# First norm: the last piece of a chunk on TensorE behind the column sums, and VectorE's pieces between tiles of h

## The chip, the cores and the metric
One core of a Trainium2 chip runs the whole program. The time is device microseconds from start to end of the program on that core; lower is better.

## The reference, cut to what matters
One layer of a hybrid decoder (256 tokens, width 2048, all float32). The part around the change is the modulation and the first norm:

```python
c_act = jax.nn.silu(c)
mod = c_act @ w_ada[l] + b_ada[l]
sh1, sc1, g1, sh2, sc2, g2 = [m[:, None, :] for m in jnp.split(mod, N_MOD, axis=-1)]
h = rms_norm(x, norm1_w[l]) * (1.0 + sc1) + sh1
proj = h @ w_in[l]
...
x = x + g1 * y_mix
h = rms_norm(x, norm2_w[l]) * (1.0 + sc2) + sh2
...
return rms_norm(x, final_norm_w)
```

`sh1` and `sc1` are a vector of 2048 times a matrix of 2048 x 4096: 32 MB that are read once and needed before the first product with `w_in` can begin.

## The kernel before
Float32 products are made of three faster ones: a weight tile is split into `whi` (ScalarE, `hi_part`) and `wlo` (VectorE, `lo_part`, `first_lo`), and h likewise, so that a unit of 256 x 512 weights is 24 matmuls on TensorE (12 of twice the width for token units). Weights come through a ring of four buffers.

The first norm is made in four chunks of 512 columns. For a chunk c the shift and scale need 16 pieces of `w_ada`, r = 0 to 15, each 128 rows x 1024 columns (shift and scale side by side, 512 KB), in a ring of 12 buffers `pc`; the DMA queue of SP brings them in order, with six units of `w_in` between. Most pieces are added on VectorE by `first_piece`: it multiplies the piece by 128 values of silu(c), one per partition, and adds it to `acc_c` (semaphore `s_pcd`). The pieces in `PE_TILES[c]` are multiplied on TensorE instead, as eight one-column matmuls with the piece as the stationary operand, accumulated in a bank (`s_pcp`). When VectorE has added its last piece, `chunk_columns(c)` on TensorE sums `acc_c` over its partitions, eight more one-column matmuls into the same bank, and sets `s_red`. VectorE's `chunk(c)` then makes the shift and the scale, ScalarE's `chunk_hi` makes `htmp0` and the high part of h for four tiles, and VectorE the low part of each.

Each chunk of h allows six units of the projections. TensorE runs units 0 to 3 of a chunk, each followed by one of its pieces of the next chunk, then the columns of the next chunk behind unit 3, and then units 4 and 5, which cover the making of the next four tiles of h. VectorE's order is written out by hand too: pieces with a `lo_part` behind r = 2, 4, 8, 11 and 15. SP issues in order and waits for a buffer's last reader. In chunk 0 there are no units yet; TensorE has the transposes of x and of parameters instead.

The lines that the text names: L886 is a piece on TensorE, L895 the column sums, L930 to L945 matmuls of units, L1320 and L1323 a piece on VectorE (the first one of a chunk, the others), L1330 to L1332 the norm's shift and scale, L1336 the low part of h, L1311 and L1340 `wlo`.

Of the kernel before, what the change touches and what calls it, by code (L numbers as in the profile page):

```python
# [17 lines left out]
KT = D // P  # L18
# [26 lines left out]
CHUNKS, CT = 4, 4  # L45
# [5 lines left out]
def unit_of(u):  # L51

    if u < EARLY_UNITS:
        return u % PER_CHUNK // 2, u // PER_CHUNK * 2 + u % 2
    return u // 8, u % 8
# [4 lines left out]


PC_RING = 12
PE_TILES = ((2, 5, 8, 11), (1, 5, 9, 13), (1, 5, 9, 13), (1, 5, 9, 13))
PC_OF_PE = [c * KT + r for c in range(CHUNKS) for r in PE_TILES[c]]
PC_OF_DVE = [i for i in range(CHUNKS * KT) if i not in PC_OF_PE]
OUT0, UP0 = PROJ_UNITS, PROJ_UNITS + 32
# [123 lines left out]
def build(nc, x, c, positions, w_ada, b_ada, norm1_w, w_in, lb_logits, gnorm_w, w_out,  # L190
# [6 lines left out]
    with ExitStack() as ctx:  # L197
# [3 lines left out]
        def sem(name):  # L201
            return ctx.enter_context(nc.semaphore(name))
# [79 lines left out]
        csilu = small[:, 0:16]  # L282
# [32 lines left out]
        s_pcp = sem("s_pcp")  # L315
# [92 lines left out]
        def ev(n):  # L408

            return 2 * n + 2  # L410
# [460 lines left out]
        def _(pe):  # L871
# [6 lines left out]
            def first_piece(i):  # L878

                c, r = i // KT, i % KT  # L880
                pe.wait_ge(s_pc[i % PC_RING], (i // PC_RING + 1) * 16)
                if r == PE_TILES[c][0]:
                    if c >= 2:
                        pe.wait_ge(s_redc, c - 1)
                for k in range(2 * CT):
                    last = pe.matmul(ps[6 + c % 2][:, k:k + 1], pc[:, i % PC_RING, k // CT, k % CT * P:(k % CT + 1) * P],  # L886
                                     csilu[:, r:r + 1], start=(r == PE_TILES[c][0] and k == 0), stop=False,
                                     skip_group_check=True)
                last.then_inc(s_pcp, 1)

            def chunk_columns(c):

                pe.wait_ge(s_pcd, sum(i < (c + 1) * KT for i in PC_OF_DVE))
                for k in range(2 * CT):
                    last = pe.matmul(ps[6 + c % 2][:, k:k + 1], acc_c[:, c % 2, k * P:(k + 1) * P], ones[:, 0:1],  # L895
                                     start=False, stop=True, skip_group_check=True)
                last.then_inc(s_red, 1)

            pe.wait_ge(s_csilu, 1)
            first_piece(2)  # L900
            for k in range(KT // 2):
                if k >= 4:
# [12 lines left out]
            for t in range(4):  # L915
                last = pe.transpose(ps[1][:, 97 + 88 * t:97 + 88 * (t + 1)], rows[0:88, 1 + t, :], ident[0:88, 0:88])
            last.then_inc(s_prmT, 1)
            first_piece(11)
            chunk_columns(0)
            pe.wait_ge(s_xTc, KT // 2)  # L920
            pe.wait_ge(s_prm, 3)

            def channel_unit(n, j, slot):

                for f in range(4):
                    out = ps[BANK[n] + f // 2][:, f % 2 * SEQ:(f % 2 + 1) * SEQ]
                    cols = slice(f * P, (f + 1) * P)
                    for k in range(UK):
                        kk = j * UK + k
                        pe.matmul(out, whi[:, slot, k, cols], h[:, kk, 0, :], start=(kk == 0 and f % 2 == 0), stop=False,  # L930
                                  skip_group_check=True)
                        pe.matmul(out, whi[:, slot, k, cols], h[:, kk, 1, :], start=False, stop=False, skip_group_check=True)  # L932
                        last = pe.matmul(out, wlo[:, slot, k, cols], h[:, kk, 0, :], start=False, stop=(kk == KT - 1),  # L933
                                         skip_group_check=True)
                last.then_inc(s_pe, 1)

            def token_unit(bank0, j, slot, hi, lo, tiles, early=None):
                for b in range(TB):
                    out, tok = ps[bank0 + b], slice(b * P, (b + 1) * P)
                    for k in range(UK):  # L940
                        kk = tiles + k
                        first, end = j == 0 and k == 0, j == 7 and k == UK - 1
                        pe.matmul(out, hi(kk, tok), whi[:, slot, k, :], start=first, stop=False)  # L943
                        pe.matmul(out, hi(kk, tok), wlo[:, slot, k, :], start=False, stop=False)  # L944
                        last = pe.matmul(out, lo(kk, tok), whi[:, slot, k, :], start=False, stop=end)  # L945
                    if early and b == 0:
                        last.then_inc(early, 1)
                last.then_inc(s_pe, 1)
# [163 lines left out]
            for u in range(PROJ_UNITS):  # L1112
                n, j = unit_of(u)
                if j == 0 and n >= EARLY:
                    pe.wait_ge(s_ev, ev(n - EARLY if n < 5 else n - 2))
                pe.wait_ge(s_lo, u + 1)
                if n < EARLY:
                    pe.wait_ge(s_h, UK * (j + 1))
                if GROUPS[n][0] in ("hi", "av", "hg"):
                    token_unit(BANK[n], j, u % RING, lambda kk, tok: h[:, kk, 0, tok], lambda kk, tok: h[:, kk, 1, tok], j * UK)  # L1120
                else:
                    channel_unit(n, j, u % RING)
                if u < EARLY_UNITS - PER_CHUNK:
                    c, t = u // PER_CHUNK + 1, u % PER_CHUNK
                    if t < 4:
                        first_piece(c * KT + PE_TILES[c][t])
                    if t == 3:
                        chunk_columns(c)
                after(u)

            def mix_hi(kk, tok):
# [127 lines left out]
        def _(dve):  # L1259
# [47 lines left out]
            def lo_part(unit, slot, ready):  # L1307

                dve.wait_ge(s_hi, unit)
                dve.wait_ge(s_pe, ready)  # L1310
                dve.tensor_tensor(wlo[:, slot], wraw[:, slot], whi[:, slot].bitcast(F32), ALU.subtract).then_inc(s_lo, 1)  # L1311

            def first_piece(i):
                c, r = i // KT, i % KT
                dve.wait_ge(s_pc[i % PC_RING], (i // PC_RING + 1) * 16)
                a, new = acc_c[:, c % 2], pc[:, i % PC_RING].rearrange("p m n -> p (m n)")
                if r == 0:
                    if c >= 2:
                        dve.wait_ge(s_red, c - 1)
                    ins = dve.tensor_scalar(a, new, csilu[:, r:r + 1], None, ALU.mult)  # L1320
                else:
                    dve.wait_ge(s_pcd, PC_OF_DVE.index(i))
                    ins = dve.scalar_tensor_tensor(out=a, in0=new, scalar=csilu[:, r:r + 1], in1=a, op0=ALU.mult, op1=ALU.add)  # L1323
                ins.then_inc(s_pcd, 1)

            def chunk(c):

                cols, sums = slice(CT * c, CT * c + CT), ps[6 + c % 2]
                dve.wait_ge(s_red, c + 1)
                st.do(dve.tensor_tensor(B1[:, cols], sums[:, 0:CT], b_shift[:, cols], ALU.add))  # L1330
                st.then(dve.tensor_tensor(acol, sums[:, CT:2 * CT], b_scale[:, cols], ALU.add))
                dve.tensor_tensor(A1[:, cols], acol, n1w[:, cols], ALU.mult).then_inc(s_redc, 1)  # L1332
                for k in range(CT * c, CT * c + CT):
                    dve.wait_ge(s_ht, k + 1)
                    dve.wait_ge(s_hhi, k + 1)
                    dve.tensor_tensor(h[:, k, 1, :], htmp0[:, k % 2], h[:, k, 0, :].bitcast(F32), ALU.subtract).then_inc(s_h, 1)  # L1336

            def first_lo(v):
                dve.wait_ge(s_hi, v + 1)
                dve.tensor_tensor(wlo[:, v], wraw[:, v], whi[:, v].bitcast(F32), ALU.subtract).then_inc(s_lo, 1)  # L1340

            dve.wait_ge(s_csilu, 1)
            for r in range(KT):
                if r not in PE_TILES[0]:
                    first_piece(r)
# [14 lines left out]
            for c in range(CHUNKS - 1):  # L1360
                v = PER_CHUNK * c
                for r in range(KT):
                    if r not in PE_TILES[c + 1]:
                        first_piece((c + 1) * KT + r)
                    if r in (2, 4, 8, 11, 15):
                        e = (2, 4, 8, 11, 15).index(r) + 2
                        if v + e < RING:
                            first_lo(v + e)
                        else:
                            lo_part(v + e + 1, (v + e) % RING, v + e - RING + 1)  # L1370
                lo_part(v + 8, (v + 7) % RING, v + 7 - RING + 1)
                if c == 1:
                    bound_logits()
                elif c == 2:
                    bound()
                chunk(c + 1)
# [368 lines left out]
```

## Time and profile before

| | us |
|---|---|
| median of 3 runs | 1317.16 (1315.12 to 1317.34) |
| profiled execution, its own time | 1316.54 |
| span of the profile | 1314.7 |
| TensorE busy | 1269.4 (97%) |
| VectorE busy | 997.6 (76%) |
| ScalarE busy | 608.1 (46%) |

The span is what the engines' records cover; the profiled execution's own time has 1.84 us around it. Busy shares are means over the whole program. The change touches only what happens in the first 135 us, so the timelines there are what is to be read. A matmul's duration in a row has the draining of its last result in it, so rows that follow each other overlap by some 0.15 us; sixteen records stand for eight float32 matmuls, in two passes each.

### The profile page before, as it was taken

The page shows a single profiled execution, that of the slowest core. Times are in us where ns is not written, and L with a number is a line of the kernel's source. Part 1 is how long each engine was busy: PE and PEld are TensorE (multiplying, and loading weights), DVE is VectorE, ACT ScalarE, POOL GpSimd, SP SyncE. Part 2 cuts the span into 40 slices and gives each one's busy share as a digit, 9 for nine tenths or more (in the row PEclk, how much of TensorE's full clock was granted, in tenths as well). Part 3 has the DMA queues.
Part 4 walks back from the last instruction along what each step waited for, and adds up shares of the span by engine and source line. Part 5 has one row for each costly group of instructions (what it writes and reads, how often), then busy time and mean ns, then how long its engine had stood idle before and what let it go on. Part 6 is the DMA issues. An engine that isn't in the chain of part 4 may idle for free.

```text
span 1314.7 us, 20785 instructions
## 1 busy us (share of the span) xinstructions
PE 1269.4 (97%) x7298; PEld 1119.3 (85%) x7298; DVE 997.6 (76%) x1278; ACT 608.1 (46%) x793; POOL 51.3 (4%) x99
## 2 busy tenths in 40 slices
PE   4799999999999999989999999999999999999997
PEld 4799999998998878878888888888888878888886
DVE  3788698998888889787878797888777765545454
ACT  3333654444545654454444444444444444434342
POOL 2000000032121000000000000000000000000000
PEclk9788999999999999989999999999999999999999
DMA  9999788888778799749777777777666675555553
GB/s 339 387 385 367 244 299 273 262 275 273 251 254 304 261 341 386 273 152 305 233 240 235 241 226 240 237 238 211 192 189 190 189 259 193 194 195 194 194 195 116
DMA packets 151715, 329.77 MB, mean 251 GB/s; under 512 B 11237, under 2 KB 11990, under 8 KB 150754
## 3 DMA queue, kind: packets, MB, share of 16 engines
q1 hardware_dynamic: 148000, 318.49, 73.1%
q0 software_dynamic: 3360, 9.98, 2.2%
q8 instruction: 40, 0.66, 0.2%
q10 hardware_dynamic: 290, 0.44, 0.1%
q14 instruction: 25, 0.20, 0.0%
HBM read 323.09 MB, written 4.19 MB: 249 GB/s over the span
## 4 chain that ended last, share of the span: by engine, by line
PE 89%; DVE 4%; DMA 3%; ACT 2%; issue 1%; SPq 1%; DVEq 0%; ACTq 0%
PE bank L1182 25%; PE bank L1188 13%; PE bank L1207 6%; PE bank L1209 6%; PE bank L1208 6%; PE bank L943 5%; PE bank L945 5%; PE bank L944 5%; PE bank L930 4%; PE bank L933 4%; PE bank L932 4%; DMA pc<-in_w_ada 3%; DVE acc_c L1323 1%; PE bank L977 1%; PE bank L964 1%
## 5 line engine op out<-in xcount | busy, mean ns | idle before, releaser
L624 ACT ACTIVATE whi<-wraw 128x1024 fp32r<-128x1024 f32 x408 | 432.0, 1060 | 630.1 <-PE bank L1188 238.9
L1311 DVE TENSOR_TENSOR wlo<-wraw,whi 128x1024 fp32r<-128x1024 f32 x404 | 494.0, 1224 | 252.3 <-ACT whi L624 250.8
L1182 PE MATMUL bank<-h,whi 128*128 128x512 f32 x1400 | 351.0, 392 | 0.0
L1182 PEld LDWEIGHTS bank<-h,whi 128*128 128x128 f32 x1400 | 252.2, 189 | 45.2
L1188 PEld LDWEIGHTS bank<-h,wlo 128*128 128x128 f32 x1400 | 191.0, 190 | 13.7
L1188 PE MATMUL bank<-h,wlo 128*128 128x256 f32 x1400 | 195.2, 282 | 0.0
L930 PE MATMUL bank<-h,whi 128*128 128x256 f32 x512 | 149.2, 291 | 3.3 <-DVE h L1336 3.3
L932 PE MATMUL bank<-h,whi 128*128 128x256 f32 x512 | 146.4, 286 | 0.0
L933 PE MATMUL bank<-h,wlo 128*128 128x256 f32 x512 | 146.3, 286 | 0.0
L1207 PE MATMUL bank<-whi,act_hi 128*128 128x512 f32 x336 | 130.8, 389 | 0.3 <-DVE evt L1599 0.3
L1209 PE MATMUL bank<-whi,act_lo 128*128 128x512 f32 x336 | 130.7, 389 | 0.0
L1208 PE MATMUL bank<-wlo,act_hi 128*128 128x512 f32 x336 | 130.7, 389 | 0.0
L1387 DVE SCALAR_TENSOR_TENSOR acc<-araw,small,acc 128x1024 f32<-128x1024 f32 x96 | 122.7, 1279 | 0.5 <-issue 0.3
L930 PEld LDWEIGHTS bank<-h,whi 128*128 128x128 f32 x512 | 99.8, 195 | 3.6 <-issue 3.4
L932 PEld LDWEIGHTS bank<-h,whi 128*128 128x128 f32 x512 | 99.9, 195 | 0.2
L933 PEld LDWEIGHTS bank<-h,wlo 128*128 128x128 f32 x512 | 99.7, 195 | 0.0
L943 PE MATMUL bank<-whi,h 128*128 128x512 f32 x192 | 81.2, 423 | 0.0
L945 PE MATMUL bank<-whi,h 128*128 128x512 f32 x192 | 77.1, 401 | 0.0
L944 PE MATMUL bank<-wlo,h 128*128 128x512 f32 x192 | 76.9, 400 | 0.0
L1207 PEld LDWEIGHTS bank<-whi,act_hi 128*128 128x128 f32 x336 | 63.1, 188 | 14.1 <-issue 1.1
L1208 PEld LDWEIGHTS bank<-wlo,act_hi 128*128 128x128 f32 x336 | 63.1, 188 | 13.2
L1209 PEld LDWEIGHTS bank<-whi,act_lo 128*128 128x128 f32 x336 | 63.1, 188 | 13.0
(233 smaller groups left out, 1325.9 us busy)
## 6 DMA issues: line engine op xcount, KB each, us to landing
wraw<-in_w_up SPq DMA_DIRECT2D x176, 512.0 KB, 4.4
araw<-in_w_ada SPq DMA_DIRECT2D x128, 512.0 KB, 5.6
wraw<-in_w_in SPq DMA_DIRECT2D x112, 512.0 KB, 4.9
wraw<-in_w_down SPq DMA_DIRECT2D x88, 512.0 KB, 4.1
pc<-in_w_ada SPq DMA_DIRECT2D x64, 512.0 KB, 11.4
wraw<-in_w_out SPq DMA_DIRECT2D x32, 512.0 KB, 6.0
x<-in_x SPq DMA_DIRECT2D x2, 1024.0 KB, 7.1
x<-in_x POOLq DMA_DIRECT2D x1, 2048.0 KB, 11.4
```

The source lines that it names most:

```text
L624: act.activation(whi[:, slot], wraw[:, slot], ACT.Copy).then_inc(s_hi, 1)
L930: pe.matmul(out, whi[:, slot, k, cols], h[:, kk, 0, :], start=(kk == 0 and f % 2 == 0), stop=False, skip_group_check=True)
L932: pe.matmul(out, whi[:, slot, k, cols], h[:, kk, 1, :], start=False, stop=False, skip_group_check=True)
L933: last = pe.matmul(out, wlo[:, slot, k, cols], h[:, kk, 0, :], start=False, stop=(kk == KT - 1), skip_group_check=True)
L943: pe.matmul(out, hi(kk, tok), whi[:, slot, k, :], start=first, stop=False)
L945: last = pe.matmul(out, lo(kk, tok), whi[:, slot, k, :], start=False, stop=end)
L1182: pe.matmul(ps[bank0 + f], whi[:, slot, k, f * P:(f + 1) * P], h[:, kk].rearrange("p a t -> p (a t)"), start=(kk == 0), stop=False, skip_g ...
L1188: last = pe.matmul(ps[bank0 + f][:, 0:SEQ], wlo[:, slot, k, f * P:(f + 1) * P], h[:, kk, 0, :], start=False, stop=(kk == KT - 1), skip_gro ...
L1207: pe.matmul(ps[bank0 + b], hi(kk, b), whi[:, slot, k, :], start=first, stop=False)
L1208: pe.matmul(ps[bank0 + b], hi(kk, b), wlo[:, slot, k, :], start=False, stop=False)
L1209: last = pe.matmul(ps[bank0 + b], lo(kk, b), whi[:, slot, k, :], start=False, stop=end)
L1311: dve.tensor_tensor(wlo[:, slot], wraw[:, slot], whi[:, slot].bitcast(F32), ALU.subtract).then_inc(s_lo, 1)
```

## The change
The pieces of TensorE are now 2, 5, 8, 15 in chunk 0 and 1, 5, 9, 15 in the others. In chunk 0 VectorE adds piece 11 and in the others piece 13, where TensorE did, and TensorE takes piece 15, where VectorE did. TensorE's last piece stands behind `chunk_columns`, no longer ahead of it. `chunk(c)` waits for that piece as well (`s_pcp`). VectorE adds piece 0 of the next chunk between tiles 1 and 2 of h, and piece 2 behind tile 3, ahead of everything else of the next chunk.

```diff
-PE_TILES = ((2, 5, 8, 11), (1, 5, 9, 13), (1, 5, 9, 13), (1, 5, 9, 13))
+PE_TILES = ((2, 5, 8, 15), (1, 5, 9, 15), (1, 5, 9, 15), (1, 5, 9, 15))
...
-                                     csilu[:, r:r + 1], start=(r == PE_TILES[c][0] and k == 0), stop=False,
+                                     csilu[:, r:r + 1], start=(r == PE_TILES[c][0] and k == 0), stop=(r == PE_TILES[c][-1]),
...
-                                     start=False, stop=True, skip_group_check=True)
+                                     start=False, stop=False, skip_group_check=True)
...
-            first_piece(11)
             chunk_columns(0)
+            first_piece(15)
...
+                    if t == 3:
+                        chunk_columns(c)
                     if t < 4:
                         first_piece(c * KT + PE_TILES[c][t])
-                    if t == 3:
-                        chunk_columns(c)
...
                 dve.wait_ge(s_red, c + 1)
+                dve.wait_ge(s_pcp, 4 * c + 4)
...
                     dve.tensor_tensor(h[:, k, 1, :], htmp0[:, k % 2], h[:, k, 0, :].bitcast(F32), ALU.subtract).then_inc(s_h, 1)
+                    if c + 1 < CHUNKS and k % CT in (1, 3):
+                        first_piece((c + 1) * KT + k % CT - 1)
...
-                    if r not in PE_TILES[c + 1]:
+                    if r not in PE_TILES[c + 1] and r not in (0, 2):
                         first_piece((c + 1) * KT + r)
```

What stands on TensorE in chunk 0 between the transposes of the parameters (L916) and the first unit, before (`s_pc11` is the landing of piece 11; `s_pcd` VectorE's sums):

```order
L886 MATMUL bank<-small,pc 128x1 [waits s_pc8]
L886 MATMUL bank<-small,pc 128x1 x7
L916 MATMUL bank<-ident,rows 128x88 [waits s_prm,s_in]
L916 MATMUL bank<-ident,rows 128x88 x3
L886 MATMUL bank<-small,pc 128x1 [waits s_pc11]
L886 MATMUL bank<-small,pc 128x1 x7
L895 MATMUL bank<-ones,acc_c 128x1 [waits s_pcd]
L895 MATMUL bank<-ones,acc_c 128x1 x7
```

The same place on TensorE now (`s_pc3` is the landing of piece 15):

```order
L886 MATMUL bank<-small,pc 128x1 [waits s_pc8]
L886 MATMUL bank<-small,pc 128x1 x7
L916 MATMUL bank<-ident,rows 128x88 [waits s_prm,s_in]
L916 MATMUL bank<-ident,rows 128x88 x3
L895 MATMUL bank<-ones,acc_c 128x1 [waits s_pcd]
L895 MATMUL bank<-ones,acc_c 128x1 x7
L886 MATMUL bank<-small,pc 128x1 [waits s_pc3]
L886 MATMUL bank<-small,pc 128x1 x7
```

The piece that stood ahead of the wait for VectorE is gone, and another stands behind the columns.

TensorE behind unit 3, ahead of the columns of chunk 1, before (`s_pc5` is piece 13 of that chunk):

```order
L933 MATMUL bank<-h,wlo 128x256
L886 MATMUL bank<-small,pc 128x1 [waits s_pc5]
L886 MATMUL bank<-small,pc 128x1 x7
L895 MATMUL bank<-ones,acc_c 128x1 [waits s_pcd]
L895 MATMUL bank<-ones,acc_c 128x1 x7
L943 MATMUL bank<-whi,h 128x512 [waits s_h,s_lo]
```

And now (`s_pc7` is piece 15 of that chunk):

```order
L933 MATMUL bank<-h,wlo 128x256
L895 MATMUL bank<-ones,acc_c 128x1 [waits s_pcd]
L895 MATMUL bank<-ones,acc_c 128x1 x7
L886 MATMUL bank<-small,pc 128x1 [waits s_pc7]
L886 MATMUL bank<-small,pc 128x1 x7
L943 MATMUL bank<-whi,h 128x512 [waits s_h,s_lo]
```

The wait for VectorE's sums now follows the unit at once, and the piece lies between the columns and unit 4.

VectorE from the last pieces of chunk 0 to the first of chunk 1, before (`s_pc2` and `s_pc3` are pieces 14 and 15 of chunk 0, `s_pc4` and `s_pc6` pieces 0 and 2 of chunk 1):

```order
L1323 SCALAR_TENSOR_TENSOR acc_c<-pc,small,acc_c 128x1024 [waits s_pcd,s_pc2]
L1340 TENSOR_TENSOR wlo<-wraw,whi 128x1024 [waits s_hi]
L1323 SCALAR_TENSOR_TENSOR acc_c<-pc,small,acc_c 128x1024 [waits s_pcd,s_pc3]
L1340 TENSOR_TENSOR wlo<-wraw,whi 128x1024 [waits s_hi]
L1330 TENSOR_TENSOR small<-bank,small 128x4 [waits s_red,s_xTc]
L1331 TENSOR_TENSOR small<-bank,small 128x4
L1332 TENSOR_TENSOR small<-small,prm 128x4 [waits s_v]
L1336 TENSOR_TENSOR h<-htmp_64,h 128x256 [waits s_hhi,s_ht] x4
L1320 TENSOR_SCALAR acc_c<-pc,small 128x1024 [waits s_pc4]
L1323 SCALAR_TENSOR_TENSOR acc_c<-pc,small,acc_c 128x1024 [waits s_pcd,s_pc6]
```

The same place now:

```order
L1323 SCALAR_TENSOR_TENSOR acc_c<-pc,small,acc_c 128x1024 [waits s_pcd,s_pc2]
L1343 TENSOR_TENSOR wlo<-wraw,whi 128x1024 [waits s_hi] x2
L1331 TENSOR_TENSOR small<-bank,small 128x4 [waits s_pcp,s_red,s_xTc]
L1332 TENSOR_TENSOR small<-bank,small 128x4
L1333 TENSOR_TENSOR small<-small,prm 128x4 [waits s_v]
L1337 TENSOR_TENSOR h<-htmp_64,h 128x256 [waits s_hhi,s_ht] x2
L1320 TENSOR_SCALAR acc_c<-pc,small 128x1024 [waits s_pc4]
L1337 TENSOR_TENSOR h<-htmp_64,h 128x256 [waits s_hhi,s_ht] x2
L1323 SCALAR_TENSOR_TENSOR acc_c<-pc,small,acc_c 128x1024 [waits s_pcd,s_pc6]
```

Piece 15 is gone from the row of sums, the norm waits for `s_pcp` too, and piece 0 of the next chunk stands in the middle of the four tiles of h.

## Rows read from the trace of the kernel before

**Rows 1.** The page, busy time of TensorE, share of the span, instructions.
```profile
PE 1269.4 (97%) x7298; PEld 1119.3 (85%) x7298; DVE 997.6 (76%) x1278; ACT 608.1 (46%) x793; POOL 51.3 (4%) x99
```

**Rows 2.** TensorE's waits, 0 to 160 us: total, times, longest.
```profile
PE bank L895 <- DVE acc_c L1323: 5.6, 3, 3.9
PE bank L930 <- DVE h L1336: 3.3, 1, 3.3
```

**Rows 3.** TensorE's timeline, chunk 0: start, duration, instruction, idle before and its releaser.
```profile
30.66 3.63 PE L886 MATMUL bank<-small,pc 128*128 128x1 f32 x32
...
34.49 2.69 PE L886 MATMUL bank<-small,pc 128*128 128x1 f32 x16
41.04 3.57 PE L895 MATMUL bank<-ones,acc_c 128*128 128x1 f32 x16 [3.86 <-DVE acc_c L1323]
47.93 0.55 PE L930 MATMUL bank<-h,whi 128*128 128x256 f32 x1 [3.32 <-DVE h L1336]
```

**Rows 4.** VectorE's timeline, end of chunk 0 and beginning of chunk 1.
```profile
33.34 2.67 DVE L1323 SCALAR_TENSOR_TENSOR acc_c<-pc,small,acc_c 128x1024 f32<-128x1024 f32 x2 [2.76 <-DMA pc<-in_w_ada]
...
37.37 1.28 DVE L1323 SCALAR_TENSOR_TENSOR acc_c<-pc,small,acc_c 128x1024 f32<-128x1024 f32 x1 [0.92 <-DMA pc<-in_w_ada]
...
39.70 1.28 DVE L1323 SCALAR_TENSOR_TENSOR acc_c<-pc,small,acc_c 128x1024 f32<-128x1024 f32 x1
...
48.34 0.43 DVE L1336 TENSOR_TENSOR h<-htmp,h 128x256 fp32r<-128x256 f32 x1 [0.56 <-ACT h L657]
...
49.66 0.75 DVE L1320 TENSOR_SCALAR acc_c<-pc,small 128x1024 f32<-128x1024 f32 x1
50.52 1.28 DVE L1323 SCALAR_TENSOR_TENSOR acc_c<-pc,small,acc_c 128x1024 f32<-128x1024 f32 x1
```

**Rows 5.** Windows of one microsecond: engines' busy time, then clock, DMA share, GB/s.
```profile
35.00:36.00 1.00, 1.00 (x9) 1.00 (x8) 1.00 (x2) 0.00 (x0) 0.00 (x0) 0.67 1.05 387
...
69.00:70.00 1.00, 0.07 (x1) 0.08 (x1) 1.00 (x2) 0.74 (x1) 0.00 (x0) 0.73 1.05 399
...
76.00:77.00 1.00, 1.00 (x5) 0.80 (x4) 0.42 (x1) 1.00 (x4) 0.00 (x0) 0.85 1.07 393
...
100.00:101.00 1.00, 1.00 (x7) 1.00 (x8) 1.00 (x2) 0.00 (x0) 0.00 (x0) 0.59 1.04 383
...
107.00:108.00 1.00, 1.00 (x5) 0.82 (x5) 0.92 (x1) 0.99 (x3) 0.00 (x0) 0.99 1.05 387
...
130.00:131.00 1.00, 1.00 (x8) 0.92 (x8) 0.97 (x3) 0.00 (x0) 0.00 (x0) 0.95 0.53 90
...
134.00:135.00 1.00, 1.00 (x6) 0.77 (x5) 0.42 (x1) 1.00 (x3) 0.71 (x2) 0.84 0.55 209
```

**Rows 6.** TensorE's timeline, the columns of chunks 1, 2 and 3.
```profile
66.82 1.84 PE L886 MATMUL bank<-small,pc 128*128 128x1 f32 x16
69.93 3.58 PE L895 MATMUL bank<-ones,acc_c 128*128 128x1 f32 x16 [1.26 <-DVE acc_c L1323]
73.36 0.77 PE L943 MATMUL bank<-whi,h 128*128 128x512 f32 x1
...
97.14 1.84 PE L886 MATMUL bank<-small,pc 128*128 128x1 f32 x16
98.85 2.34 PE L895 MATMUL bank<-ones,acc_c 128*128 128x1 f32 x16
...
126.22 1.84 PE L886 MATMUL bank<-small,pc 128*128 128x1 f32 x16
128.53 1.95 PE L895 MATMUL bank<-ones,acc_c 128*128 128x1 f32 x16 [0.47 <-DVE acc_c L1323]
```

**Rows 7.** VectorE's timeline, the last pieces of chunk 1 and of chunk 3.
```profile
65.81 4.06 DVE L1323 SCALAR_TENSOR_TENSOR acc_c<-pc,small,acc_c 128x1024 f32<-128x1024 f32 x3
...
125.81 2.67 DVE L1323 SCALAR_TENSOR_TENSOR acc_c<-pc,small,acc_c 128x1024 f32<-128x1024 f32 x2 [1.42 <-DMA pc<-in_w_ada]
```

**Rows 8.** SP's queue, issues of pieces 8 to 11 of chunk 2.
```profile
74.05 6.07 SPq L439 DMA_DIRECT2D pc<-in_w_ada  x4
```

## The prediction
> **What bounds the kernel now.** I read the page first: TensorE is busy 97% of the span [rows 1], so what counts is when its continuous work begins and what is lost inside it. Next the waits of TensorE up to 160 us [rows 2]: after the start it waits four times, three times for the sums on VectorE ahead of `chunk_columns` (5.6 us, longest 3.9) and once for the first tiles of h (3.3 us). The timelines give their places. In chunk 0 the pieces 5 and 8 run at full speed, piece 11 is the last of TensorE's work (done at 37.18), then it sits idle 3.86 us, takes 3.57 us for the column sums and idles 3.32 us more until h is there at 47.93 [rows 3]. In chunk 1 it idles 1.26 us by the bracket (1.4 us by its rows, 68.5 to 69.93), in chunk 3 0.47 us; in chunk 2 the columns start with no wait [rows 6]. From 47.93 on everything else is work, so a microsecond by which unit 0 or a later resumption moves is a microsecond of the end.
>
> VectorE is paced by landings in chunk 0: it waits for pieces 12 and 14 [rows 4], and each piece lands 1.35 us behind the one before (524 KB at 387 GB/s, [rows 5]). In chunk 1 it is late and paced by its own work: its last three pieces run back to back to 69.87 [rows 7], while piece 15 had landed about 22 transfers behind piece 14 of chunk 0, at 37.4 + 22 x 1.35 = 67.1.
>
> The third thing to see is the granted clock. It fell (shares of one-microsecond rows worked out) at 35.3, 69.5, 100.2 and 130.9, and was full again at 76.3, 107.0 and 134.3 [rows 5]. Ahead of each fall TensorE had left its wide matmuls for one-column ones: pieces at 30.66 [rows 3], 66.82, 97.14 and 126.22 [rows 6]. So it fell 4.7, 2.6, 3.0 and 4.7 us after they ended. At 35.3 it had not been idle at all. At full speed eight one-column matmuls take 1.7 us of the queue, at half 3.43 (69.93 to 73.36, [rows 6]).
>
> **The change part by part.** Pieces of VectorE: twelve a chunk before and after; it loses 15 and gets 11 or 13. TensorE has four a chunk, as before. The `stop` flags are no instructions; I cost them at nothing.
>
> *Chunk 0.* Piece 11 moves into VectorE's idle 2.76 us ahead of 33.34 [rows 4]: 1.28 us of work, covered. (Uncovered it would cost 1.28.) Its last piece is now 14, which starts on its landing at 37.37 and ends at 38.65; the columns began 0.06 us behind the last sum, so they start at 38.71 instead of 41.04, a gain of 2.33. But the new wait on `s_pcp` makes the norm wait for piece 15 on TensorE behind them, and the clock is at half there: columns 3.43, piece 3.57, end 45.71, against 41.04 + 3.57 = 44.61. **+1.10 us** for the norm, h, unit 0. Queued behind that wait are the norm's three small operations and h, whose reader is unit 0.
>
> Here a rule bears on the cost. By the columns at half clock, sixteen loads and matmuls take 3.57 us [rows 3]. The Trainium skill, TensorE: Matmul & The Clock Gate, section LDWEIGHTS (loading the stationary operand), gives a load as the number of columns divided by 1.2 in ns, with no clock in it; an estimate from it is 16 x 107 ns = 1.7 us for a piece at any clock. By it the two would end at 42.1 and the norm would come 2.5 us earlier. The trace agrees at full clock (1.84) and contradicts it at half, so the row is taken.
>
> *VectorE between tiles.* After h tile 1 it idles about 0.56 us until tile 2; piece 0 (0.75 us) goes there, so tile 2 slips about 0.2 us and tile 3 hardly. Units 0 and, later, the two units that cover a norm don't need tile 2 that early. Behind h the next piece starts where piece 0 did: 50.52 - 49.66 = **0.86 us** gained on VectorE [rows 4], in chunks 1 to 3.
>
> *Chunk 1.* VectorE ends its last piece at 69.87 + 1.10 - 0.86 = 70.11. TensorE ends unit 3 at 66.82 + 1.10 = 67.9, has no piece 13 to fill the wait, idles 2.3 us and starts the columns at 70.17. Columns and piece 15 take 3.4 us at full clock and 6.9 at half. If the clock falls 2.6 to 4.7 us after 67.9, that is 0.4 to 2.4 us into them: 4.5 to 6.5 us; I take 5.4. TensorE resumes wide work at 75.6 instead of 73.36: **+2.2 us**, the 1.10 included. After resuming, the clock stayed at half for 2.9, 5.9 and 3.9 us in chunks 1, 2, 3 [rows 5, 6], so the luck of chunk 1 was good; a mean of 4.3 costs 2.1 instead of 1.5: **+0.65**.
>
> *Chunk 2.* TensorE is now 2.9 us late, VectorE 2.2 - 0.86 = 1.3. The columns had no wait and get none; columns plus piece are the same sixteen matmuls in the other order. **0.**
>
> *Chunk 3.* Its 0.47 us of idle is gone, since TensorE arrives 2.9 us later and piece 14 lands at 125.81 as before [rows 6, 7]. **-0.47.**
>
> *Queue.* A piece 11 of the next chunk reuses the buffer of piece 15, so SP waits for TensorE there. In chunk 2 four issues run from 74.05 to 80.12, the last from about 78.6 [rows 8]; TensorE is done with piece 15 by 75.6 to 77. Hidden by 1.6 us or more; beyond that it would cost the DMA stream what is missing.
>
> Sum: 2.2 + 0.65 - 0.47 = +2.4 us. Profiled execution: 1316.54 + 2.4 = 1318.9. It lies 0.62 under the median shown, so for the median **1319.5 us**. Both ends: chunk 1 all at full clock gives 3.4 in place of 5.4 (-2.0), all at half 6.9 (+1.5); the recoveries are between 2.9 and 5.9 us, which is 0.75 us each way per chunk, some 1.5 for three.
>
> **The rivals.**
> *A, the forecast* (chance 0.50): as above, 1318.0 to 1321.
>
> *B, the series in chunk 1 runs wholly at half clock* (0.22). For it: the fall before came 0.5 us ahead of the columns. Resumption at 77.1, +3.7; with recovery and the idle gone, +3.9: 1321.1. If the buffer wait also bites by a microsecond, 1322.
>
> *C, it runs wholly at full clock* (0.18). For it: two falls came 4.7 us late, and TensorE is wide 1.1 us longer. Resumption at 73.7, +0.3; +0.65 - 0.47: 1317.6. Against it: 2.3 us of idle lie in the stretch.
>
> *D, faster: the longer unbroken run on TensorE restores the clock* (0.10). From 38.71 to 45.7 it is busy without a break; if the clock came back where the piece begins, the piece would take 1.8: the norm at 44.0, -0.6, and units 0 to 3 at full. VectorE's chain is then the bound in chunk 1, and ends at 69.87 - 0.6 - 0.86 = 68.4; the series at full takes 3.4 us more, resumption at 71.9 and no slow stretch behind it: -3.0 in all, with the 0.47: 1313.7. It decides if the clock is full before 43 us. Against it: it fell at 35.3 during such matmuls, and before it stayed at half through 3.57 us of them.
> The Trainium skill, same page, section What's actually happening, says that activity releases the throttle; by that alone D would be right, and the run from 30.66 to 37.18 here speaks against counting these matmuls as such activity.
>
> A second way to no gain, that the change does nothing, is excluded: VectorE's last sum is on the chain in chunk 0.
>
> **How the numbers follow.** Within 0.2% (2.6 us, about what a measurement of this kernel tells from no change) is 1314.5 to 1319.8. Faster: D, 0.10. Same: C and just over half of A, 0.46. Slower: B and the rest of A, 0.44. The range, 1315.5 to 1322.5, leaves out most of D and the end of B with the buffer wait.
>
> **What would show it.** Right: columns at about 38.7 in two groups to 45.7, unit 0 near 49.0; piece 0 between tiles 1 and 2 of h; an idle of 2 to 2.5 us ahead of the columns in chunk 1 and TensorE back at 75 to 76; no wait in chunks 2 and 3. Wrong: a clock at full in chunk 0's columns (D), VectorE waiting for a landing in chunk 1, an SP queue that stands still for `s_pcp`, or a wait of unit 1 for tile 2 of h.

## The result and the profile after

The changed kernel takes 1319.28 us (median of 20 runs, 1317.51 to 1321.46) against 1317.02 before (20 runs, 1314.24 to 1318.85). The ratio is 1.0016, with a 95% interval of 1.0010 to 1.0022: slower by 2.3 us. That is clear of noise over 20 runs and lies within the 0.2% that the prediction counted as "same". The forecast was 1319.5. The profiled execution took 1318.94 us with a span of 1317.1, which is 2.4 longer than the span before.

TensorE's timeline of the changed kernel (start, duration, instruction, idle before it and what ended it); it answers to [rows 3, 6]:

```profile
38.73 3.57 PE L895 MATMUL bank<-ones,acc_c 128*128 128x1 f32 x16 [1.86 <-DVE acc_c L1323]
42.16 3.55 PE L886 MATMUL bank<-small,pc 128*128 128x1 f32 x16
49.06 0.55 PE L930 MATMUL bank<-h,whi 128*128 128x256 f32 x1 [3.35 <-DVE h L1337]
...
70.20 2.23 PE L895 MATMUL bank<-ones,acc_c 128*128 128x1 f32 x16 [1.59 <-DVE acc_c L1323]
72.29 3.55 PE L886 MATMUL bank<-small,pc 128*128 128x1 f32 x16
75.70 0.77 PE L943 MATMUL bank<-whi,h 128*128 128x512 f32 x1
...
99.89 1.95 PE L895 MATMUL bank<-ones,acc_c 128*128 128x1 f32 x16 [0.29 <-DVE acc_c L1323]
101.69 2.89 PE L886 MATMUL bank<-small,pc 128*128 128x1 f32 x16
...
129.51 1.95 PE L895 MATMUL bank<-ones,acc_c 128*128 128x1 f32 x16 [0.25 <-DVE acc_c L1323]
131.31 1.93 PE L886 MATMUL bank<-small,pc 128*128 128x1 f32 x16
```

Every column group now starts a series of two: L895, then L886, 3.4 us from start to start at half clock and 1.8 at full. In chunk 0 the columns start 2.3 us earlier than before, but the series ends later, and unit 0 comes at 49.06 instead of 47.93. In chunk 1 unit 4 comes at 75.70 instead of 73.36.

VectorE's timeline, which answers to [rows 4, 7]; first the norm before, then the rows of the changed kernel:

```profile
44.72 0.16 DVE L1330 TENSOR_TENSOR small<-bank,small 128x4 f32<-128x4 f32 x1 [2.60 <-PE bank L895]
```

```profile
45.85 0.16 DVE L1331 TENSOR_TENSOR small<-bank,small 128x4 f32<-128x4 f32 x1 [4.91 <-PE bank L886]
...
48.83 0.75 DVE L1320 TENSOR_SCALAR acc_c<-pc,small 128x1024 f32<-128x1024 f32 x1
49.49 0.42 DVE L1337 TENSOR_TENSOR h<-htmp,h 128x256 fp32r<-128x256 f32 x1
50.45 0.42 DVE L1337 TENSOR_TENSOR h<-htmp,h 128x256 fp32r<-128x256 f32 x1 [0.55 <-ACT h L657]
50.80 1.28 DVE L1323 SCALAR_TENSOR_TENSOR acc_c<-pc,small,acc_c 128x1024 f32<-128x1024 f32 x1
...
66.09 4.05 DVE L1323 SCALAR_TENSOR_TENSOR acc_c<-pc,small,acc_c 128x1024 f32<-128x1024 f32 x3
...
125.40 4.05 DVE L1323 SCALAR_TENSOR_TENSOR acc_c<-pc,small,acc_c 128x1024 f32<-128x1024 f32 x3
```

The norm (L1331) is now released by L886, the piece on TensorE, and starts at 45.85 instead of 44.72. Piece 0 of the next chunk stands between tiles of h, and tile 3 still waits for ScalarE, so VectorE loses nothing by it. The last sum of chunk 1 ends at 66.09 + 4.05 = 70.14. In chunk 3 the last three pieces run back to back to 129.45: VectorE is paced by itself there and no longer by a landing.

Windows of one microsecond; the third number from the end is the granted clock. They answer to [rows 5]:

```profile
40.00:41.00 1.00, 1.00 (x6) 1.00 (x6) 0.94 (x1) 0.00 (x0) 0.00 (x0) 0.50 1.02 377
43.00:44.00 1.00, 1.00 (x6) 1.00 (x6) 0.00 (x0) 0.00 (x0) 0.00 (x0) 0.50 1.06 389
...
71.00:72.00 1.00, 1.00 (x10) 1.00 (x9) 1.00 (x2) 0.00 (x0) 0.00 (x0) 0.86 1.04 397
78.00:79.00 1.00, 1.00 (x5) 0.82 (x4) 0.44 (x3) 1.00 (x3) 0.00 (x0) 0.73 1.09 393
...
136.00:137.00 1.00, 1.00 (x4) 0.79 (x4) 0.44 (x2) 1.00 (x3) 0.71 (x2) 0.72 0.04 8
```

The clock stays at half (0.50, the 1.2 GHz level) through the whole series of chunk 0, although TensorE is busy without a break. In chunk 1 it falls at 71.7, inside the columns, and is full again at 78.5; behind chunk 3 it is full again at 136.6.

### The profile page after: what moved, and what is told of

The parts are those of the page before. It is cut to its first block, busy times and chain, and to the rows that moved or that the text cites. A ratio compares the mean times of both kernels' runs of the same rounds, so it can differ in the third digit from the quotient of the medians.

```text
span 1317.1 us, 20788 instructions
## 1 busy us (share of the span) xinstructions
PE 1273.9 (97%) x7298; PEld 1123.2 (85%) x7298; DVE 996.5 (76%) x1278; ACT 608.3 (46%) x793; POOL 51.4 (4%) x99
## 4 chain that ended last, share of the span: by engine, by line
PE 86%; DVE 6%; issue 3%; ACT 2%; DMA 2%; SPq 0%; DVEq 0%; ACTq 0%
PE bank L1182 24%; PE bank L1188 13%; PE bank L1207 6%; PE bank L1209 6%; PE bank L1208 6%; PE bank L943 5%; PE bank L945 5%; PE bank L944 5%; PE bank L932 3%; PE bank L930 3%; PE bank L933 3%; DVE acc_c L1323 3%; DMA pc<-in_w_ada 2%; PE bank L977 1%; PE bank L964 1%
```

## Experiments

Twelve kernels, each timed beside the kernel before. Medians of 11 or 12 runs (e2 has 5, e7 6, the changed kernel 20) and ratios with 95% intervals. The kernel before, timed with each, had medians from 1316.83 to 1317.91, so between two rows of this table a microsecond by the medians is not clear of noise:

| kernel | median us | ratio to the kernel before |
|---|---|---|
| changed kernel | 1319.28 | 1.0016 [1.0010, 1.0022] |
| e1 between only | 1317.50 | 1.0004 [0.9995, 1.0013] |
| e2 no between | 1322.13 | 1.0042 [1.0028, 1.0055] |
| e3 chunk 0 alone | 1317.35 | 1.0002 [0.9993, 1.0011] |
| e4 chunk 0 as before | 1318.27 | 1.0014 [1.0005, 1.0023] |
| e5 piece ahead | 1317.12 | 1.0002 [0.9993, 1.0011] |
| e6 warm chunk 0 | 1316.88 | 0.9996 [0.9987, 1.0005] |
| e7 warm all | 1321.83 | 1.0037 [1.0025, 1.0049] |
| e8 warm, late loads | 1319.43 | 1.0016 [1.0007, 1.0025] |
| e9 ahead, warm | 1316.88 | 0.9998 [0.9989, 1.0007] |
| e10 ahead, warm, late load | 1315.16 | 0.9982 [0.9973, 0.9990] |
| e11 fill the wait | 1319.95 | 1.0017 [1.0009, 1.0026] |
| e12 ahead, late load | 1315.82 | 0.9990 [0.9981, 0.9999] |

### The parts of the change, one at a time

**e1: the kernel before, with VectorE's pieces between the tiles of h.**

```diff
+                    if c + 1 < CHUNKS and k % CT in (1, 3):
+                        first_piece((c + 1) * KT + k % CT - 1)
...
-                    if r not in PE_TILES[c + 1]:
+                    if r not in PE_TILES[c + 1] and r not in (0, 2):
```

> The kernel before with only VectorE's pieces 0 and 2 moved between and behind the tiles of h. My theory: VectorE's last sum of chunk 1 comes 0.86 us earlier, at 69.0, and TensorE's idle time there shrinks from 1.4 to 0.6 us, but the gain is not kept: in chunk 3 the last sum waits for the landing of piece 15 at 127.1, so the wait there grows instead. Time 1316.5 to 1317.0, the time before being 1317.0. Rival: the earlier sum is kept to the end, 1316.1. Second rival: tile 2 of h slips and TensorE waits for it, 1317.6 or more.

Measured 1317.50, half a microsecond above my range and not told apart from no change. TensorE's timeline of this kernel, chunks 1 to 3:

```profile
69.57 1.95 PE L895 MATMUL bank<-ones,acc_c 128*128 128x1 f32 x16 [0.91 <-DVE acc_c L1323]
...
98.73 2.88 PE L895 MATMUL bank<-ones,acc_c 128*128 128x1 f32 x16 [1.46 <-DVE acc_c L1323]
...
128.46 1.98 PE L895 MATMUL bank<-ones,acc_c 128*128 128x1 f32 x16 [0.43 <-DVE acc_c L1323]
```

In chunk 1 TensorE is ahead of the kernel before (its chunk 0 was 0.5 us late in this execution, by a later landing), and then it waits 1.46 us in chunk 2, where it had not waited. In chunk 3 the columns start at 128.46, against 128.53 [rows 6]: where the landings put them. What is gained ahead of that point is not kept.

**e2: the changed kernel without that move** (the two lines of the last diff taken out).

> The changed kernel without the move of VectorE's pieces 0 and 2: they stand behind the four tiles of h again. My theory: the last sum of chunk 1 comes 0.86 us later than in the changed kernel, near 71.0, and there is no slack to take it, 1320.1. Rival: the pieces between the tiles cost something themselves, then this is as fast as the changed kernel or faster, 1319.0.

Measured 1322.13: 2.85 us slower than the changed kernel. Both guesses missed: the sign was my theory's, the size three times as large. TensorE's timeline in chunk 1, and two windows of one microsecond ahead of it:

```profile
71.32 3.58 PE L895 MATMUL bank<-ones,acc_c 128*128 128x1 f32 x16 [3.19 <-DVE acc_c L1323]
74.75 3.55 PE L886 MATMUL bank<-small,pc 128*128 128x1 f32 x16
78.17 0.77 PE L943 MATMUL bank<-whi,h 128*128 128x512 f32 x1
```

```profile
69.00:70.00 1.00, 0.00 (x0) 0.00 (x0) 0.90 (x2) 0.75 (x1) 0.00 (x0) 1.00 0.80 270
70.00:71.00 1.00, 0.00 (x0) 0.00 (x0) 1.00 (x1) 0.00 (x0) 0.00 (x0) 0.64 1.04 397
```

VectorE's last sum is 1.12 us later than in the changed kernel: 0.86 by the order, 0.26 because this execution's chunk 0 was that much later. TensorE's idle stretch is longer, 3.19 us against 1.59. The clock falls at 70.3, before the columns begin, and all sixteen matmuls run at half: 6.85 us where the changed kernel had 5.50. Unit 4 comes 2.47 us later, and behind it the clock stays at half for 5.7 us, against 2.8 in the changed kernel. In this pair of executions the clock amplified the delay of VectorE.

**e11: the same kernel with the wait of chunk 1 filled** by 12 matmuls of 128 columns, whose results nothing reads:

```diff
+            def warm(n, bank_no):
+                for _ in range(n):
+                    pe.matmul(ps[bank_no][:, 256:256 + P], x0[:, 0, 0:P], diag0[:, 0], start=True, stop=True)
...
                     if t == 3:
+                        if c == 1:
+                            warm(12, 6)
                         chunk_columns(c)
```

> The kernel without VectorE's pieces between the tiles (1322.1), with 12 extra matmuls in TensorE's wait ahead of the columns of chunk 1. It tells what made that kernel 2.8 us slower than the changed one, where VectorE's order is worth 0.86. My theory: the longer idle time makes the clock fall ahead of the columns, so all sixteen one-column matmuls run at half. With the wait filled the clock holds to the columns or beyond: 3.5 to 5 us for columns and piece instead of 6.9, unit 4 at 75 to 76.5 instead of 78.2, the end at 1319.3 to 1320.5. Rival: the idle time is not the cause: unit 4 at 78.2 and 1322.

Measured 1319.95, 2.2 us less by the medians; the ratios, 1.0017 and 1.0042, have intervals that do not touch. TensorE's timeline:

```profile
68.15 2.84 PE L901 MATMUL bank<-diag,x 128*128 128x128 f32 x24
71.51 1.95 PE L895 MATMUL bank<-ones,acc_c 128*128 128x1 f32 x16 [0.51 <-DVE acc_c L1329]
73.31 3.06 PE L886 MATMUL bank<-small,pc 128*128 128x1 f32 x16
76.23 0.77 PE L947 MATMUL bank<-whi,h 128*128 128x512 f32 x1
```

The columns start no earlier (71.51) but run at full clock in 1.8 us, and unit 4 is back at 76.23 instead of 78.17. The clock falls at 73.9 instead of 70.3. Work that computes nothing made the kernel faster; the idle time ahead of the columns is what costs. The two profiled executions don't show the gain at their end: both took 1321.12 us, and how long the clock stays at half in the later chunks differs from one execution to the next. The 2.2 us rest on the medians, the mechanism on the rows of chunk 1.

**e4: the changed kernel with chunk 0 as before.**

```diff
-PE_TILES = ((2, 5, 8, 15), (1, 5, 9, 15), (1, 5, 9, 15), (1, 5, 9, 15))
+PE_TILES = ((2, 5, 8, 11), (1, 5, 9, 15), (1, 5, 9, 15), (1, 5, 9, 15))
...
-            chunk_columns(0)
-            first_piece(15)
+            first_piece(11)
+            chunk_columns(0)
```

> The changed kernel with chunk 0 as before: pieces 2, 5, 8, 11 on TensorE, the columns last, piece 15 on VectorE. My theory: the norm of chunk 0 comes 1.1 to 1.2 us earlier, at 44.7, and all of it reaches the columns of chunk 1, which start at 69.1, and the end: 1318.2. Rival: chunk 0 is covered and the loss is all in chunks 1 to 3: 1319.3, no change.

Measured 1318.27, by the medians 1.0 us less than the changed kernel, which is the number that I gave; the two ratios, 1.0014 and 1.0016, have intervals that overlap, so the rival is not excluded. TensorE's timeline:

```profile
69.07 3.16 PE L895 MATMUL bank<-ones,acc_c 128*128 128x1 f32 x16 [2.04 <-DVE acc_c L1323]
72.10 3.55 PE L886 MATMUL bank<-small,pc 128*128 128x1 f32 x16
```

The columns of chunk 1 start 1.13 us earlier, as expected. But the wait ahead of them is longer (2.04 against 1.59 us), the clock falls at 69.6, and unit 4 comes at 75.51, only 0.19 us earlier than in the changed kernel. "All of it reaches the end" is not what this trace shows.

**e3: the kernel before with the change in chunk 0 alone.**

```diff
-PE_TILES = ((2, 5, 8, 11), (1, 5, 9, 13), (1, 5, 9, 13), (1, 5, 9, 13))
+PE_TILES = ((2, 5, 8, 15), (1, 5, 9, 13), (1, 5, 9, 13), (1, 5, 9, 13))
...
-            first_piece(11)
             chunk_columns(0)
+            first_piece(15)
...
+                dve.wait_ge(s_pcp, 4 * c + 4)
```

> The kernel before with the change in chunk 0 alone: piece 11 on VectorE, columns, then piece 15 on TensorE; chunks 1 to 3 and VectorE's order between tiles of h as before. My theory: the norm comes 1.1 to 1.2 us later, at 45.8, VectorE's last sum of chunk 1 at 71.0, and the wait of 0.47 us in chunk 3 takes part of it: 1317.7. Rival: chunk 0 costs nothing, 1317.0.

Measured 1317.35, which does not tell my 1317.7 from 1317.0. Its trace shows unit 0 at 48.73, so the chunk still pays there; in chunk 3 TensorE waits 1.36 us again. So the change of chunk 0 costs nothing that can be told from noise where the later chunks are as before (0.1 us by this median), and by the median of e4 about a microsecond, not clear of noise either, where they are changed.

**e5: the changed kernel with piece 15 ahead of the columns in chunks 1 to 3.**

```diff
-                    if t == 3:
-                        chunk_columns(c)
                     if t < 4:
                         first_piece(c * KT + PE_TILES[c][t])
+                    if t == 3:
+                        chunk_columns(c)
```

> The changed kernel with TensorE's piece 15 of chunks 1 to 3 ahead of the columns instead of behind them; chunk 0 as changed. My theory: the piece then runs in the wait for VectorE's sums. Columns of chunk 1 at 70.2 as in the changed kernel, unit 4 at 72.5 to 73.6 instead of 75.7, and the end 2.0 to 2.5 us earlier: 1317.0. Rival: the order does not matter, since the stretch of one-column matmuls has the same length and the clock falls in it either way: 1319.3.

Measured 1317.12, 2.2 us less than the changed kernel. TensorE's timeline:

```profile
68.39 1.84 PE L886 MATMUL bank<-small,pc 128*128 128x1 f32 x16
70.09 2.07 PE L895 MATMUL bank<-ones,acc_c 128*128 128x1 f32 x16
72.03 0.77 PE L943 MATMUL bank<-whi,h 128*128 128x512 f32 x1
...
97.43 2.14 PE L886 MATMUL bank<-small,pc 128*128 128x1 f32 x16 [1.38 <-DMA pc<-in_w_ada]
...
127.17 1.95 PE L886 MATMUL bank<-small,pc 128*128 128x1 f32 x16 [0.36 <-DMA pc<-in_w_ada]
```

In chunk 1 the piece fills the wait for VectorE exactly, and unit 4 comes at 72.03, earlier than before the change (73.36). The clock falls at 71.7 here as in the changed kernel, so the gain is the filled wait and not the clock. In chunks 2 and 3 TensorE now waits for the landing of piece 15. The position behind the columns cost as much as the whole change (2.2 us of 2.3).

### The price of the clock in chunk 0, and what bounds chunk 3

**e6: the changed kernel with 40 such matmuls in TensorE's idle time of chunk 0** (`warm(8, 7)` between pieces 5 and 8, `warm(14, 7)` ahead of the columns, `warm(18, 7)` behind piece 15).

> The changed kernel with 40 extra 128-column matmuls into unused columns of a bank in TensorE's idle time of chunk 0: 8 between pieces 5 and 8, 14 ahead of the columns, 18 behind piece 15. My theory: the price of chunk 0 is the clock. With the clock at full, columns and piece 15 take 3.5 us instead of 7.1, the norm starts at 42.3, unit 0 at 45.7. The end gains less: VectorE's sums of chunk 1 come at 67.2, from its landings, and chunk 3 is paced by the landing of piece 14 at 125.8: 1316.7 to 1318. Rival: the pieces take 3.5 us at any clock or the clock falls all the same: 1319.3.

Measured 1316.88, 2.4 us less. TensorE's timeline in chunk 0 and at the columns of chunk 1, and one window:

```profile
36.64 3.32 PE L901 MATMUL bank<-diag,x 128*128 128x128 f32 x28
39.80 1.84 PE L895 MATMUL bank<-ones,acc_c 128*128 128x1 f32 x16
41.51 1.93 PE L886 MATMUL bank<-small,pc 128*128 128x1 f32 x16
43.30 5.89 PE L901 MATMUL bank<-diag,x 128*128 128x128 f32 x36
...
67.91 1.95 PE L895 MATMUL bank<-ones,acc_c 128*128 128x1 f32 x16 [1.88 <-DVE acc_c L1330]
```

```profile
41.00:42.00 1.00, 1.00 (x11) 1.00 (x11) 0.30 (x1) 0.00 (x0) 0.00 (x0) 1.00 1.06 387
```

At full clock columns and piece take 3.5 us instead of 7.0. The fourteen matmuls overshot the wait by 0.7 us (VectorE's last sum ended at 39.03), and the last eighteen ran at half for a time (43.6 to 47.0) and held unit 0 to 48.94, about where it had been. Yet VectorE got its norm 2.3 us earlier, and the columns of chunk 1 start at 67.91. The clock was also full again ahead of unit 0 and not only at 54.6, so TensorE's first piece of chunk 1 comes at 51.90 instead of 54.32. The 2.4 us are the worth of both.

**e7: 20 more ahead of the columns of chunks 1 and 2.**

```diff
                     if t == 3:
+                        if c < 3:
+                            warm(20, 7 - c % 2)
                         chunk_columns(c)
```

> As the kernel with extra matmuls in chunk 0, and 20 more in TensorE's wait ahead of the columns of chunks 1 and 2. My theory: columns and piece at full clock there too, 3.5 us, unit 4 at 71 to 72; the landing of piece 14 of chunk 3 holds all at 125.8, so TensorE resumes at 130.6 to 131 instead of 133.1: 1315.5 to 1317. Rival: the clock is not the price, the extra matmuls only add work: 1320 or more.

A miss, 1321.83, where the rival had it (1320 or more). TensorE's timeline:

```profile
67.01 4.63 PE L901 MATMUL bank<-diag,x 128*128 128x128 f32 x40
71.48 1.84 PE L895 MATMUL bank<-ones,acc_c 128*128 128x1 f32 x16
...
99.00 4.63 PE L901 MATMUL bank<-diag,x 128*128 128x128 f32 x40
```

Twenty of them take 4.5 us, more than the waits that they were to fill (1.88 us in chunk 1 and 0.49 in chunk 2 of e6), so they stand on the path. The clock did hold through the columns. So this run says nothing for or against the price of the clock.

**e8: and four loads of chunk 3 moved behind its last piece**, with `chunk_hi(3)` and the `lo_part` calls of units 16 to 19 reordered to match:

```diff
-                    if r % 4 == 3:
+                    if n < 2 and r % 4 == 3:
                         load_in(PER_CHUNK * n + RING + r // 4)
+                if n == 2:
+                    for j in range(4):
+                        load_in(PER_CHUNK * n + RING + j)
```

> As the last kernel, and the loads of four units that are needed only behind chunk 3 moved behind its last piece, with their splitting and the norm of chunk 3 reordered on ScalarE and VectorE to match. My theory: with TensorE early, the landings of chunk 3 are the bound; three loads fewer ahead of them land piece 15 at 123.1 instead of 127.1, TensorE resumes at 127 to 128: 1312 to 1314. Rival: TensorE's own work ahead of chunk 3 is the bound and the loads give nothing: as the last kernel.

Measured 1319.43, far from my 1312 to 1314. It shares the oversized extra matmuls. Its columns of chunk 3 start at 130.88 with no wait at all, so TensorE's own work was the bound and not the landings. How much of its 2.4 us against e7 comes from the loads, and how much from a shorter slow stretch in chunk 0, these two don't tell.

**e9: e5 with 8, 9 and 8 extra matmuls in chunk 0, sized to the idle time.**

> The changed kernel with piece 15 ahead of the columns in chunks 1 to 3, and 25 extra matmuls in chunk 0 sized to fit: 8 between pieces 5 and 8, 9 ahead of the columns, 8 behind piece 15. My theory: columns at 38.8 and piece 15 at full clock, norm at 42.4, unit 0 at 45.7. TensorE is then ahead of the landings of piece 15, which come at 97.1 and 127.1 in chunks 2 and 3 whatever TensorE does, so it waits 2 us or more in each and the end is where it was with the piece ahead alone: 1316.5 to 1317.2. Rival: the earlier start is kept to the end: 1313.5 to 1315.

Measured 1316.88: against e5 (1317.12) the earlier start gained nothing that can be told from noise. TensorE's timeline at the pieces 15:

```profile
67.44 1.95 PE L886 MATMUL bank<-small,pc 128*128 128x1 f32 x16 [2.76 <-DMA pc<-in_w_ada]
...
97.18 1.95 PE L886 MATMUL bank<-small,pc 128*128 128x1 f32 x16 [0.34 <-DMA pc<-in_w_ada]
...
127.06 1.95 PE L886 MATMUL bank<-small,pc 128*128 128x1 f32 x16 [0.49 <-DMA pc<-in_w_ada]
```

TensorE is early in all three chunks and waits for the piece each time, though by less than the 2 us that I gave for chunks 2 and 3: the wait in chunk 1 had taken most of it.

**e10: e9 with one load moved in chunks 2 and 3.**

```diff
-                    if r % 4 == 3:
-                        load_in(PER_CHUNK * n + RING + r // 4)
+                    if r % 4 == 3 and not (n and r == 11):
+                        load_in(PER_CHUNK * n + RING + r // 4 - (n > 0 and r == 15))
+                if n:
+                    load_in(PER_CHUNK * n + RING + 3)
```

> As the kernel with piece 15 ahead and 25 extra matmuls, and in chunks 2 and 3 the load of the third unit moved behind piece 15 on SP's queue. My theory: piece 15 lands one transfer, 1.36 us, earlier in chunks 2 and 3, and since the landings are the bound, the end comes 1.3 us earlier: 1315.4. Rival: the landings are no bound: no change against the kernel without the moved load.

**e12: the same load moved, without the extra matmuls.**

> The changed kernel with piece 15 ahead of the columns in chunks 1 to 3 and the load of the third unit moved behind piece 15 in chunks 2 and 3; no extra matmuls. My theory: without the moved load TensorE waited 1.4 us for the landing of piece 15 in chunk 2 and 0.4 us in chunk 3; with it those waits go and the end comes up to 1.3 us earlier, 1315.8 to 1316.5. Rival: TensorE must also be early, with the extra matmuls in chunk 0, for the load to be worth anything: 1317.1.

Measured 1315.16 and 1315.82; both beat the changed kernel and the kernel before, e12 the latter narrowly (the interval of its ratio ends at 0.9999). Of TensorE's waits between 60 and 160 us this is all that is left in e10 (the first row) and in e12 (the second; waiting instruction, what it waited for, total, times, longest):

```profile
PE bank L888 <- DMA pc<-in_w_ada: 3.2, 1, 3.2
```

```profile
PE bank L897 <- DVE acc_c L1325: 0.8, 1, 0.8
```

Each has one wait in chunk 1 and none in chunks 2 and 3. The landings of piece 15 were the bound there: moving the load took 1.7 us off e9 (e10) and 1.3 off e5 (e12).

## Why the prediction was right, point by point

- **Chunk 0, +1.10 for the norm.** Measured: columns at 38.73 (38.71 forecast), norm at 45.85 against 44.72 in the timeline before, unit 0 at 49.06 (49.03). The clock stayed at half, and e6 shows that this is the price of the norm: at full the series took 3.5 us. How much of the end this part is stays open: 1.0 us by the medians with e4, 0.1 with e3, neither clear of noise.
- **A piece's price by clock.** The rule from the Trainium skill (TensorE: Matmul & The Clock Gate, LDWEIGHTS) gives an estimate of 1.7 us a piece at any clock. The rows after give 3.4 us at half (72.29 to 75.70) and, for eight such matmuls at full, 1.8 (99.89 to 101.69): the rows decide against it at half.
- **VectorE gains 0.86.** Last sum of chunk 1 at 70.14 (70.11). The direct term was right. What I did not work out is what it protects: e2 puts 2.85 us on its absence. In its trace the longer idle stretch ends with the clock at half ahead of the columns, and e11 got 2.2 us back by filling it.
- **Chunk 1, +2.2 at the resumption.** Measured +2.34: columns at 70.20 (70.17), the series 5.50 us (5.4). The choice between full and half was near the mean of its bounds, and the execution fell there; that is luck. The idle time ahead of the columns was 1.6 us by the bracket and not the 2 to 2.5 that I named as a sign: TensorE ended unit 3 at 68.45 and not at 67.9, since the clock in chunk 0 was full again at 54.6 and not at 52.4 as before. The columns wait for VectorE, so their start did not change by it. e5 shows the part that the order has in it.
- **Recovery, +0.65.** Not in this execution: half for 2.8 us behind the resumption, as before. It is a mean, and the profile is one draw; in the traces of e2 and e4 the same stretch was 5.7 and 4.3 us.
- **Chunk 2, no wait, 0.** Missed: 0.29 us of wait and a series of 4.56 us instead of 3.9, with the slow stretch behind it 1.2 us shorter than before in return. TensorE came out of it 0.58 us further behind.
- **Chunk 3, -0.47.** Mis-sized: 0.25 us of wait remains, and the chunk gave back 0.10 us in all. VectorE was by then paced by its own work (last sum 129.45), not by the landing at 125.8 that I took.
- **Rivals.** B (all at half) and C (all at full) are the ends that the clock chose among; e2 ran like B. D did not happen: the clock stayed at half through 7 us of one-column matmuls. The longer wait for the buffer of piece 15 did not show: VectorE and TensorE had no longer wait for a landing in chunks 2 and 3.

The sum came out at +2.4 forecast, +2.4 in the profiled spans and +2.3 in the medians, but not term by term. TensorE's first one-column matmuls behind each chunk (chunks 1 and 2; behind chunk 3 the first matmul of the next unit) show how far the changed kernel was behind:

| behind | before, us | changed, us | late by |
|---|---|---|---|
| chunk 1 | 83.16 | 85.46 | 2.30 |
| chunk 2 | 112.24 | 115.12 | 2.88 |
| chunk 3 | 137.50 | 140.28 | 2.78 |
| end of the span | 1314.7 | 1317.1 | 2.4 |

The forecast had 2.85, 2.85 and 2.38 in the first three rows. The recovery of chunk 1 was put 0.7 us too high, its resumption 0.14 too low, chunks 2 and 3 together 0.95 too low, and 0.4 us came back behind 140 us, where the two kernels have the same work. So the place of the loss and the terms of chunk 0 and of the series in chunk 1 were right, and the agreement to a tenth is luck.

## What to carry to other kernels

Ask of an operation that is moved from one engine to another whether it now fills a wait or lies behind it. Piece 15 behind the columns instead of ahead of them cost 2.2 us (changed kernel against e5), with the same instructions. Where an engine's speed depends on what it did last, a wait can cost more than its length, and filling it with dummy work of about its size pays (e11), while oversizing it costs: e7, with 4.5 us put into waits of 1.9 and 0.5, was 5.0 us slower than e6. And when a gain early in a pipeline disappears, look for the next thing that arrives by its own clock, here a landing at 127 us: once the order of the loads was changed by one transfer, a gain came through.

## What the runs showed of the hardware

- One-column float32 matmuls back to back did not bring the clock back: at 0.50 through 7 us of them, with TensorE busy all the time. The Trainium skill (TensorE: Matmul & The Clock Gate, What's actually happening) says that activity releases the throttle; for these matmuls the rows decide otherwise. For the 128-column ones they agree: in e6 the clock was full up to 43.6, and having fallen it was back at 47.0, during the last eighteen.
- A wait ahead of such matmuls can cost more than its length: in e2 against the changed kernel VectorE's last sum was 1.12 us later, TensorE's idle time 1.6 us longer and the series behind it 1.35 us longer, by the clock.
- VectorE stands still for 0.52 us ahead of the same sum of chunk 1 in the traces of before, after and e1. By the pace of the landings (1.35 us a piece, an estimate from [rows 5]) its piece was there some microseconds earlier. What it waits for stays open; it stays with the instruction where that comes earlier (at 56.02 in e9) or later (59.76 in e2; 58.64 in the changed kernel).
